# The opening of a three-layer kernel's third layer: gate rows and two tiles from an unnormalised source

## The reference, cut to what matters

```python
x = x + rms_norm(y_mlp, norm_mlp_post)          # end of layer two
h = rmsnorm_3(x, norm_g)                        # x * rsqrt(mean(x*x)) * norm_g
proj = h @ w_in                                 # 14352 columns
aq, ak, av, ao, az, ai, af, ..., bf, ... = split(proj)
q, k = split(silu(causal_depthwise_conv(concat(aq, ak), conv_w)))   # 4 taps
b = cumsum(log_sigmoid(af + ml_bf));  i = ai + ml_bi                # 4 heads
# per head: stabiliser m_t = max over s of (b_t - b_s + i_s), weights exp(...), products with q, k, v
```

## Time and profile before

| | |
|---|---|
| timed runs, median of 3 | 2835.09 us (2832.41 to 2835.9) |
| the profiled execution's own time | 2828.44 us |
| its span (first to last instruction) | 2826.4 us |
| PE busy | 2662.1 us, 94% of the span |
| DVE busy | 1517.4 us, 54% |
| ACT busy | 988.6 us, 35% |
| granted PE clock, mean over the span | 0.964 |
| HBM read | 288.79 MB |
| chain that ended last, by engine | PE 60%, DVE 6%, ACT 3% |

### The profile page before, as it was taken

The page is one execution under the profiler, slowest core; times in us unless marked ns, Lnnn a source line. Parts: engine busy times, 40 slices in busy tenths (PEclk is TensorE's granted clock), DMA queues, the critical chain, the costliest instruction groups (busy, mean ns, idle before and its releaser), DMA issues.

```text
span 2826.4 us, 30173 instructions
## 1 busy us (share of the span) xinstructions
PE 2662.1 (94%) x12198; PEld 1986.2 (70%) x12198; DVE 1517.4 (54%) x2830; ACT 988.6 (35%) x1700; POOL 15.3 (1%) x20
## 2 busy tenths in 40 slices
PE   7989999979997999989999999979989999999998
PEld 5867677633445566668778888758778878778786
DVE  5347655457765398965344544556543233344534
ACT  3234445321213232224233332245744244432222
POOL 0000000000000000000000000000000000000000
PEclk9889999989998999999999999989999999999999
DMA  4311001299973210212213222122212432213120
GB/s 152 81 44 48 31 31 60 91 398 393 413 319 95 79 28 25 90 60 82 98 61 119 90 90 90 46 75 72 77 60 82 108 79 78 87 60 112 68 90 30
DMA packets 178750, 296.02 MB, mean 105 GB/s; under 512 B 26160, under 2 KB 120752, under 8 KB 170416
## 3 DMA queue, kind: packets, MB, share of 16 engines
q1 hardware_dynamic: 175088, 282.52, 28.6%
q0 software_dynamic: 2304, 8.39, 0.8%
q10 hardware_dynamic: 1216, 3.15, 0.3%
HBM read 288.79 MB, written 4.19 MB: 104 GB/s over the span
## 4 chain that ended last, share of the span: by engine, by line
PE 60%; DVE 6%; ACT 3%; issue 1%; DVEq 0%; ACTq 0%
PE ps L317 16%; PE ps L319 16%; PE ps L318 16%; PE ps L325 6%; PE ps L2007 2%; PE ps L331 1%; DVE ps L1932 1%; PE ps L340 1%; PE ps L2104 1%; PE ps L2034 0%; PE ps L384 0%; DVE x L2270 0%; DVE arena L2267 0%; DVE t L355 0%; ACT L2710 0%
## 5 line engine op out<-in xcount | busy, mean ns | idle before, releaser
L303 DVE TENSOR_TENSOR ws0l<-w,ws0h 128x1024 fp32r<-128x1024 f32 (+1 forms) x125 | 135.8, 1087 | 134.1 <-ACT ws0h L295 132.2
L303 DVE TENSOR_TENSOR ws1l<-w,ws1h 128x1024 fp32r<-128x1024 f32 (+2 forms) x125 | 134.9, 1080 | 131.2 <-ACT ws1h L295 131.1
L295 ACT ACTIVATE ws1h<-w 128x1024 fp32r<-128x1024 f32 (+2 forms) x125 | 117.3, 938 | 147.6 <-PE ps L319 142.0
L303 DVE TENSOR_TENSOR ws2l<-w,ws2h 128x1024 fp32r<-128x1024 f32 (+1 forms) x93 | 104.7, 1126 | 99.1 <-ACT ws2h L295 99.0
L295 ACT ACTIVATE ws0h<-w 128x1024 fp32r<-128x1024 f32 (+1 forms) x125 | 117.9, 943 | 103.8 <-PE ps L319 103.8
L1932 DVE SCALAR_TENSOR_TENSOR ps<-arena,ps 128x512 f32<-128x512 f32 x224 | 150.9, 749 | 0.0
L325 PE MATMUL ps<-arena 128*128 128x512 f32 (+11 forms) x440 | 134.7, 482 | 1.6 <-ACT t L752 1.1
L317 PE MATMUL ps<-hpc_hi,ws1h 128*128 128x512 f32 x320 | 128.1, 400 | 6.1 <-DVE ws1l L303 4.0
L317 PE MATMUL ps<-hpc_hi,ws2h 128*128 128x512 f32 x328 | 130.8, 399 | 1.5 <-issue 1.5
L319 PE MATMUL ps<-hpc_hi,ws2l 128*128 128x512 f32 x328 | 128.8, 393 | 0.0
L318 PE MATMUL ps<-hpc_lo,ws2h 128*128 128x512 f32 x328 | 128.8, 393 | 0.0
(11 more groups left out here) (564 smaller groups left out, 6182.3 us busy)
## 6 DMA issues: line engine op xcount, KB each, us to landing
w<-in_w_gate_up SPq DMA_DIRECT2D x32, 2048.0 KB, 12.3
w<-in_w_in SPq DMA_DIRECT2D x37, 1024.0 KB, 5.4
w<-in_w_down SPq DMA_DIRECT2D x32, 1024.0 KB, 12.7
w<-in_w_ff SPq DMA_DIRECT2D x16, 2048.0 KB, 8.2
w<-in_w_in SPq DMA_DIRECT2D x13, 2048.0 KB, 8.3
w<-in_w_in SPq DMA_DIRECT2D x48, 512.0 KB, 5.2
w<-in_w_branch SPq DMA_DIRECT2D x6, 2048.0 KB, 7.8
w<-in_w_out SPq DMA_DIRECT2D x4, 2048.0 KB, 7.6
```

Source lines behind the costliest of these rows:

```text
L295: A_(e).activation(pair_of(t)[0], tiles[t][1], ACT.Copy).then_inc(*e.inc(hi, ("hi", t)))
L303: e.go.tensor_tensor(p[1], tiles[t][1], p[0].bitcast(F32), ALU.subtract).then_inc(*e.inc(lo, ("lo", t)))
```

## The change

1. **A second split source.** `hpU` = `x` times `norm_g_3`, without the norm's factor, split into high (ACT) and low (DVE) block by block inside `add_norm`. It lies over `hb3[0]` (96 KB) and `y3` (112 KB), so heads 0 and 2 now use `hb3[1]`, and 1 and 3 `hb3[0]`.
2. **Gate rows and tiles q0, q1 of head 0 from `hpU`.** PE interleaves the Gram blocks of `x(k)` with six narrow matmuls of block k-1. The Gram bank is now `ps2`. The factor is a function of the token alone, so it multiplies the results instead: a copy `r9` of the row is made (ACT), and DVE multiplies the 12 rows, the 4 rows and the two tiles by it (`take`, which replaces ACT's eviction of q0 and q1). `pe_spread(n9)` stands in the middle of tile q0.
3. **The gate chain between the blocks of `hp3`.** `hp3` is still built for all other tiles; the functions `between(k)` put pieces of the chain, two `take`s and the splits of q2 and q3 between its blocks. q2 reads `hp3` block by block.
4. **Splits earlier.** `tile_end` lets the gate tile and q0 be split during the feed-forward, and q1 behind the Gram's diagonal; SP loads two more slabs before it waits in `gates_sp`.
5. **First tap on ACT.** For all 16 query and key tiles the convolution's first tap is an ACT copy with a scale instead of a DVE operation.
6. In step -1 the row comes behind q5 instead of in front of it.

```diff
-        n9 = Norm("n9", 8, D, tm[0], tm[1:3], roots[0], ps[6])
+        n9 = Norm("n9", 8, D, tm[0], tm[1:3], roots[0], ps[2])
+        r9 = tm[2]
...
-            for k in range(8):
-                e.wait_ge(*dv(("x8", k)))
-                pe_gram(e, n9, k, x[:, k, :])
-            pe_spread(e, n9)
...
-            e.tile_end = F_END - 1
+            e.tile_end = tG + 1
...
             act_root(e, n8)
+            for k in range(8):
+                e.wait_ge(*dv(("x8", k)))
+                e.go.activation(hpU[0][:, k, :], x[:, k, :], ACT.Copy, scale=vcol("norm_g_3", k)).then_inc(*e.inc(ev, ("hpU", k)))
             act_root_of(e, n9)
...
+            def lowU(k):
+                e.wait_ge(*ev(("hpU", k)))
+                e.go.scalar_tensor_tensor(out=hpU[1][:, k, :], in0=x[:, k, :], scalar=vcol("norm_g_3", k),
+                                          in1=hpU[0][:, k, :].bitcast(F32), op0=ALU.mult, op1=ALU.subtract).then_inc(*e.inc(dv, ("hpU", k)))
+            add_norm(e, n8, yF, "norm_mlp_post_2", "x8", lowU)
             dve_diagonal(e, n9)
+            e.tile_end = len(tiles) - 1
+            dve_lo(e, tG + 2)
             dve_recip(e, n9)
-            dve_row(e, n9)
...
+        hpU = (at("hpu_hi", 96 * KB, [P, 8, 512], F32R), at("hpu_lo", 112 * KB, [P, 8, 512], F32R))
...
+            def rows(k):
+                e.wait_ge(*dv(("hpU", k)))
+                for j, (c0, m) in enumerate(((0, 4), (4, 12))):
+                    e.go.matmul(ps[j][0:m, :], gate_hi[:, k, c0:c0 + m], hpU[0][:, k, :], start=k == 0, stop=False)
+                    e.go.matmul(ps[j][0:m, :], gate_hi[:, k, c0:c0 + m], hpU[1][:, k, :], start=False, stop=False)
+                    i = e.go.matmul(ps[j][0:m, :], gate_lo[:, k, c0:c0 + m], hpU[0][:, k, :], start=False, stop=k == 7)
+                    if k == 7:
+                        i.then_inc(*e.inc(mm, ("tile", tG) if j else "ig"))
...
+            for k in range(8):
+                e.wait_ge(*dv(("x8", k)))
+                pe_gram(e, n9, k, x[:, k, :])
+                if k:
+                    rows(k - 1)
+            rows(7)
...
-            norm_split_act(e, hp3, "hp3", tm[4:7])
+            e_ = tm[1]
+
+            def between(k):
+                if k == 1:
+                    act_hi(e, tG + 3)
+                if k == 3:
+                    e.wait_ge(*dv("zf"))
+                    e.go.activation(e_[0:12, :], tm[0][0:12, :], ACT.Abs).then_inc(*e.inc(own_a))
+                    e.wait_ge(*e.last)
+                    e.go.activation(e_[0:12, :], e_[0:12, :], ACT.Exp, scale=-1.0).then_inc(*e.inc(ev, "zexp"))
+                if k == 5:
+                    act_hi(e, tG + 4)
+                if k == 6:
+                    e.wait_ge(*dv("z1"))
+                    e.go.activation(e_[0:12, :], e_[0:12, :], ACT.Ln).then_inc(*e.inc(ev, "zln"))
+
             e.tile_end = len(tiles) - 1
             act_hi(e, tG + 2)
-            e_ = tm[1]
-            e.wait_ge(*dv("zf"))
-            e.go.activation(e_[0:12, :], tm[0][0:12, :], ACT.Abs).then_inc(*e.inc(own_a))
-            e.wait_ge(*e.last)
-            e.go.activation(e_[0:12, :], e_[0:12, :], ACT.Exp, scale=-1.0).then_inc(*e.inc(ev, "zexp"))
-            e.wait_ge(*dv("z1"))
-            e.go.activation(e_[0:12, :], e_[0:12, :], ACT.Ln).then_inc(*e.inc(ev, "zln"))
+            e.wait_ge(*mm(("n9", "row")))
+            e.go.activation(r9[:], n9.bank[:], ACT.Copy).then_inc(*e.inc(ev, "r9"))
+            norm_split_act(e, hp3, "hp3", tm[4:7], between)
+
+        def floor_act(e):
...
-            norm_split_dve(e, n9, "norm_g_3", hp3, "hp3", tm[4:7])
-            e.tile_end = len(tiles) - 1
-            dve_lo(e, tG + 2)
             g, z, e_ = e.go, tm[0], tm[1]
+
+            def take(q):
+                e.wait_ge(*mm(("tile", ml_t[0][q])))
+                g.tensor_tensor(raws[q][:, 3:515], SM.bank(q, 0)[:], r9[:], ALU.mult).then_inc(*e.inc(dv, ("M", "ev", q, 0)))
+
+            def between(k):
+                if k == 1:
+                    e.wait_ge(*in_g3("g3"))
+                    e.wait_ge(*mm(("tile", tG)))
+                    step(g.tensor_tensor(z[0:12, :], ps[1][0:12, :], r9[0:12, :], ALU.mult))
+                    step(g.tensor_scalar(z[0:12, :], z[0:12, :], gb3[0:12, 1:2], None, ALU.add), "zf")
+                if k == 2:
+                    dve_lo(e, tG + 3)
+                if k == 3:
+                    take(0)
+                if k == 5:
+                    e.wait_ge(*ev("zexp"))
+                    step(g.tensor_scalar(e_[0:12, :], e_[0:12, :], 1.0, None, ALU.add), "z1")
+                    take(1)
+                if k == 6:
+                    dve_lo(e, tG + 4)
+
             g.memset(raws[0][:, 0:3], 0.0).then_inc(*e.inc(own_v))
             g.memset(raws[1][:, 0:3], 0.0).then_inc(*e.inc(dv, "pad3"))
-            e.wait_ge(*in_g3("g3"))
-            e.wait_ge(*mm("ig"))
-            step(g.tensor_scalar(ig[0:4, :], ps[0][0:4, :], gb3[0:4, 0:1], None, ALU.add))
-            e.wait_ge(*mm(("tile", tG)))
-            step(g.tensor_scalar(z[0:12, :], ps[1][0:12, :], gb3[0:12, 1:2], None, ALU.add), "zf")
-            e.wait_ge(*ev("zexp"))
-            step(g.tensor_scalar(e_[0:12, :], e_[0:12, :], 1.0, None, ALU.add), "z1")
+            e.wait_ge(*ev("r9"))
+            norm_split_dve(e, n9, "norm_g_3", hp3, "hp3", tm[4:7], between)
+            step(g.tensor_tensor(ig[0:4, :], ps[0][0:4, :], r9[0:4, :], ALU.mult))
+            step(g.tensor_scalar(ig[0:4, :], ig[0:4, :], gb3[0:4, 0:1], None, ALU.add))
...
-        plan_m, NM = plan3(4, (0, 1, 2, 3, 4, "row", 5, "v0", "v1"), ((0, 1), (2, 3), (4, "row"), (5, "v0")), ("v1",))
+        plan_m, NM = plan3(4, (0, 1, 2, 3, 4, 5, "row", "v0", "v1"), ((0, 1), (2, 3), (4, "row"), (5, "v0")), ("v1",))
         unit3 = [(hh, i) for hh in range(8) for i in (3, 2, 1, 0)]
+
+        EARLY = (("M", "ev", 0, 0), ("M", "ev", 1, 0))
...
+            def row9(k):
+                if k == 4:
+                    pe_spread(e, n9)
+                return dv(("hpU", k))
...
-                    buf, n = hb3[hh % 2], P * (i + 1)
+                    buf, n = hb3[(hh + 1) % 2], P * (i + 1)
...
+                        src, arrived = hp3, None
+                        if hh == 0 and q < 2:
+                            src = hpU
+                        if hh == 0 and q in (0, 2):
+                            arrived = row9 if q == 0 else lambda k: dv(("hp3", k))
+                        pe_tile(e, ml_t[hh][q], SM.bank(q, hh)[:], src, arrived)
...
+                    if hh == 0 and q == 5:
+                        floor_act(e)
+                    if ("M", "ev", q, hh) not in EARLY:
+                        e.wait_ge(*mm(("tile", ml_t[hh][q])))
...
+                        r, o, ch = raws[q % 2], hb3[(hh + 1) % 2][:, q, :], channel(hh, q)
+                        if ("M", "ev", q, hh) not in EARLY:
+                            e.wait_ge(*dv("pad3"))
+                            e.wait_ge(*dv(("M", "cv", hh, q - 2) if q >= 2 else ("M", "cv", hh - 1, q + 2)))
+                            e.go.activation(r[:, 3:515], b[:], ACT.Copy).then_inc(*e.inc(ev, ("M", "ev", q, hh)))
+                        e.wait_ge(*SM.took(("M", "ev", q, hh)))
+                        e.wait_ge(*mm(("M", "s", 4 * hh - 5)))
+                        e.go.activation(o, r[:, 0:512], ACT.Copy, scale=conv3[:, ch, 0:1]).then_inc(*e.inc(ev, ("M", "tap0", q, hh)))
...
-                            ch = 2 * hh + q if q < 2 else 8 + 2 * hh + q - 2
-                            r, o = raws[q % 2], hb3[hh % 2][:, q, :]
-                            e.wait_ge(*ev(("M", "ev", q, hh)))
-                            e.wait_ge(*mm(("M", "s", 4 * hh - 5)))
-                            e.go.tensor_scalar(o, r[:, 0:512], conv3[:, ch, 0:1], None, ALU.mult).then_inc(*e.inc(own_v))
+                            r, o, ch = raws[q % 2], hb3[(hh + 1) % 2][:, q, :], channel(hh, q)
+                            e.wait_ge(*ev(("M", "tap0", q, hh)))
                             for k in range(1, 4):
-                                e.wait_ge(*e.last)
+                                if k > 1:
+                                    e.wait_ge(*e.last)
...
-            load_slabs(e, S3)
+            load_slabs(e, S3 + 2)
```

More of the change, by code:

```diff
@@ L2274, in add_norm, with norm_split_dve @@
                 then(7)
-        def norm_split_dve(e, N, gain, hp, tag, bufs):
+        def norm_split_dve(e, N, gain, hp, tag, bufs, then=None):
             def low(k):
@@ L2287, in norm_split_dve, with norm_split_act @@
                     low(k - 1)
+                if then is not None:
+                    then(k)
             low(7)
-        def norm_split_act(e, hp, tag, bufs):
+        def norm_split_act(e, hp, tag, bufs, then=None):
             for k in range(8):
@@ L2503, in gates_pe @@
             e.wait_ge(*lo(("lo", tG)))
-            for j, (c0, m) in enumerate(((0, 4), (4, 12))):
-                for k in range(8):
```

(13 more changed lines are left out.)

18 lines of the change are left out of this document (7 added, 11 removed).

## The result

The changed kernel took 2826.09 us (median of 8 runs, 2823.34 to 2829.7) against 2833.46 us before (8 runs, 2831.55 to 2835.9): ratio 0.9975, 95% interval 0.9965 to 0.9986. By the ratio that is 7.1 us less, between 4.0 and 9.9; the medians differ by 7.4. The forecast was 2826.5 us, range 2821 to 2834.

A forecast was written before the change was run, and what follows sets the result against it. Behind an opening bound by a DVE and ACT chain, everything is PE's. q4's start at 1879.2 plus 7.1, 1.6 and 7.5 put first scores at 1895.4 against 1904.0 us; 2835.09 - 8.6 = 2826.5 us, range 2821 to 2834.

The forecast's parts named there:

- the opening: Stretch up to head 0's first scores, a chain through DVE and ACT: scores at 1895.4 against 1904.0 us, 8.6 less.
- The first scores as the one point that counts: Start of head 0's first scores, 1904.0 us before: if it comes earlier by d, the rest follows by d.
- the base, 2835.09: Time the gain was subtracted from: timed runs' median, 6.65 us above the one execution's 2828.44 us.
- Gate rows' end: Gram blocks and gate rows in turn on PE, 2.29 us per block: end at 1844.4 us, before 1861.8.
- Reciprocal: Norm factor behind q1's split: ready at 1846.1, PE's spread at 1847.1 us, so hidden with 1.0 us to spare.
- Waits behind exponential and logarithm: DVE's waits for high parts queued on ACT behind gate chain operations: 0.6 us, bounds 0 and 3.8.
- q4 itself: Tile q4 on PE after an idle wait: 7.13 us, not 5.44.
- the 5 that I had named as a sign of being right: PE idle for 5 us or more in front of q4, released by DVE's ws0l; about 7 us was expected.
- Taps: First tap of 16 convolutions moved from DVE to ACT: counted 0, bounds -7.0 and +11.2 us.
- Rival B: ACT's insertions hold the gate chain: 3.8 us of waits instead of 0.6, gain 4.4, time 2830.7 us; chance 0.14.
- E: Clock stays at 1.2 GHz in the mixed stretch of Gram blocks and gate rows: 27.1 us for 15.1, time 2838.5; chance 0.04.
- the sum that decides: DVE from the first block of hp3 to the gate chain's end: 24.5 us, chain ends at 1873.3, only 1.0 earlier.

The follow-up runs named there:

- e5: Changed kernel with the splits of q4 and q5 early and both tiles writing to banks that stand empty; 2826.89 us, ratio to before 0.9982.
- e9: Changed kernel with q0 and q1 computed from hp3 again and the gate chain's pieces behind hp3; 2826.52 us, ratio to before 0.9976.
- e12: e9 plus free banks for q4 and q5, q4's split early and the floor's exponential moved; 2826.62 us, ratio to before 0.9979.
- e1: Changed kernel with the first tap of all 16 convolutions back on DVE; 2825.2 us, ratio to before 0.9969.
- e2: Changed kernel with the gate chain's pieces behind the last block of hp3 again; 2829.14 us, ratio to before 0.9984.
- e7: Changed kernel with q0 and q1 computed from hp3 again, without DVE's two takes; 2825.09 us, ratio to before 0.9968.
- e8: Combined version (free banks, q0's low part later, floor early) with first taps on ACT only in head 0, DVE in later heads; 2820.34 us, ratio 0.9952.

## Why the prediction was right

**The quantity.** 8.6 us were forecast for the opening, 7.45 came, and the time fell by 7.1 to 7.4. The first scores as the one point that counts held in the large: seam and time moved together from 2829 (86.3) to 2819 us (75). It did not hold for small steps: e5, e9 and e12 have seams 1.8 to 2.3 us shorter than the changed kernel's and medians 0.4 to 0.8 us longer, which the times can't tell from nothing.

**Luck.** The forecast of 2826.5 us lies 0.4 from the median of 2826.09 because two errors cancel: the base, 2835.09, was the median of three runs and 1.6 us above that of eight (2833.46), and the gain was put 1.2 to 1.5 us too high. What the prediction earned is the gain to within those 1.5 us, not the 0.4.

**Step by step** (new trace less 7.67; forecast in brackets). Last accumulation 1816.4 (1816.45). `add_norm` 1822.3 (1822.35). Clock up at 1829.9 (1829.3). Gate rows' end 1845.1 (1844.4): the clock rose 0.6 later. Reciprocal 1.3 us ahead of PE's spread (1.0): hidden. `hp3` begins 1849.6 (1848.8). Waits behind exponential and logarithm 0.72 (0.6). End of the chain 1873.8 (1873.3). q4 1879.7 (1879.2).

**What was off.** Of the missing 1.15 us, 0.5 is q4's later start; 0.7 is q4 itself, which took 7.86 and not 7.13. The idle time ahead of it was 4.76 and not 7, just under the 5 that I had named as a sign of being right, as PE finished q3 at 1874.9 and not 1872. The waits in q2 were 2.9 us in three pieces, and q3 behind them, for which I had counted 5.44, took 7.0 with the granted clock at 0.74. It cost nothing, for PE was early.

**Taps.** I had put 0 on them between -7.0 and +11.2. They cost 0.9 us in the heads and give 0.5 in the opening. The Trainium skill (ScalarE: Activation LUTs, section "Rules for kernel authors") keeps multiplications on VectorE; the traces agree that the operation is dearer on ACT, 0.72 us in the changed kernel against 0.48 in e1, and that in the heads VectorE is the better place, by 0.9 us in 173.

**Table loads.** The exponential starts 0.01 us after its table load, the logarithm 0.02. The drain of 1.38 us of the Trainium skill (ScalarE: Activation LUTs, section "What ACT_TABLE_LOAD costs") isn't seen here either. Rival B asked for 3.8 us of waits, and 0.72 came, because DVE had the split and the `take`s to do meanwhile; left uncovered, as in e2 and e7, the waits were 3.02 and 2.46. E is excluded by the clock: 1.00 from 1840 to 1850.

**What I had not seen.** I called DVE's stretched chain "the sum that decides". As written it decides, through q4, and 24.5 us were forecast for it where 24.3 passed. But the stretching was itself a choice of the change, and e9, which does without it, has a seam 2.3 us shorter, if not a shorter time. The prediction took the change as one block; it asked what each edit costs, and not what the time would be without it.

**Open.** With its taps on DVE, e1 passes from first scores to the next stage in 172.8 us, and the kernel before, with the same taps, in 174.3. The waits there differ (one at L752 is 1.57 before and 0.41 in e1), but the 1.5 us lie in the clock: ahead of the next stage's first eviction PE took 7.3 us at a granted 0.77 before, and 5.7 at 1.00 in e1. The same tile took 7.3 in e7, e8 and e9 too, so the taps' place doesn't decide it; what does was not tried. Nor was it why the stretch from 100 to 300 us varies by several us between executions of the same code.

## What to carry to other kernels

Work that needs no normalised input is worth pulling ahead of a norm when the engine that waits is the one that bounds the kernel; but interleaving a serial chain with the producer of the next tiles can delay that producer by as much as it hides, so try each part alone and both ways. A wait can have several causes in a row (a low part, a bank, a small exponential behind silus): free one and the next one names itself as the releaser, and the gain comes only with the last. Two small operations that fill a round trip to another engine were free here (e7), and taking them out won nothing.
